# Norm sums added tile by tile under the projection slabs, in a two-layer hybrid block and a third block on one core

## The reference

```
def hybrid_layer(x, ...):
    z = rms_norm(x, norm_g) @ w_in
    y_conv = conv_module(...) @ w_conv_out          # 31 taps over time, LayerNorm, silu
    y_ret  = retention_branch(...) @ w_ret_out      # 4 heads, 256 x 512 each
    y_attn = window_attention_branch(...) @ w_attn_out
    merged = g[:, :, 0] * y_conv + g[:, :, 1] * y_ret + g[:, :, 2] * y_attn
    return x + merged @ w_out

def second_block(x, ...):
    h = _layer_norm(x, ln0_g, ln0_b)
    u_r, v_r, q_r, f_r, i_r, g_r, ga_r, gb_r = split(h @ w_in + b_in)
    y_a = _gmlp_spatial_gate(gelu(u_r), gelu(v_r), ...)   # LayerNorm over gelu(v_r)
    y_b = _hgrn2(q_r, f_r, i_r, g_r, ...)                 # 8 heads
    merged = sigmoid(ga_r) * (y_a @ w_a) + sigmoid(gb_r) * (y_b @ w_b)
    h1 = _layer_norm(ALPHA * h + merged @ w_o, ln1_g, ln1_b)
    ffn = (silu(h1 @ w_ffn_gate) * (h1 @ w_ffn_up)) @ w_ffn_down
    ple = sigmoid(h1 @ w_ple_gate + b_ple_gate) * (p @ w_ple)
    return _layer_norm(ALPHA * h1 + ffn + ple, ln2_g, ln2_b)
```

## Time and profile before

| what | us |
|---|---|
| median of 3 runs (3377.92 to 3380.22) | 3378.5 |
| the profiled execution | 3380.46 |
| its span | 3378.7 |
| TensorE busy in it | 3233.1 (96%) |
| VectorE, ScalarE, GpSimd busy | 1661.4, 1130.7, 1320.7 |
| mean granted TensorE clock | 0.98 of full |

### The profile page before, as it was taken

One profiled execution on the slowest core, in us unless ns is written; L12 is line 12 of the kernel. 1 busy time (PEld: TensorE's weight loads), 2 busy tenths in 40 slices (PEclk: granted clock), 3 DMA queues, 4 the chain that ended last, 5 costly groups with the idle time before them and its releaser, 6 DMA issues.

```text
span 3378.7 us, 42669 instructions
## 1 busy us (share of the span) xinstructions
PE 3233.1 (96%) x14040; PEld 2523.7 (75%) x14040; DVE 1661.4 (49%) x2500; ACT 1130.7 (33%) x1623; POOL 1320.7 (39%) x966
## 2 busy tenths in 40 slices
PE   7999999999999899999999999998999999999998
PEld 5866776767888686776776788876878787688885
DVE  5964565465344397575556544146562152331213
ACT  3232333355332222332235634224454232232222
POOL 3433433411555253433342145442334344254542
PEclk9999999999999999999999999998999999999999
DMA  4212222200322222221221032231112222132221
GB/s 150 97 63 68 87 66 71 71 29 29 122 100 93 96 102 67 88 69 67 75 75 44 26 106 94 99 118 49 63 68 75 87 88 93 62 100 98 94 98 70
DMA packets 73172, 272.07 MB, mean 81 GB/s; under 512 B 8128, under 2 KB 9152, under 8 KB 72384
## 3 DMA queue, kind: packets, MB, share of 16 engines
q1 hardware_dynamic: 69984, 252.74, 22.3%
q10 hardware_dynamic: 3072, 17.82, 1.5%
HBM read 264.24 MB, written 8.39 MB: 81 GB/s over the span
## 4 chain that ended last, share of the span: by engine, by line
PE 90%; DVE 5%; ACT 2%; DVEq 2%; issue 1%; DMA 0%; ACTq 0%; POOL 0%; SPq 0%; POOLq 0%
PE gem L296 22%; PE gem L298 22%; PE gem L297 22%; PE xp L382 4%; PE xp L541 2%; PE xp L372 2%; PE gem L504 2%; PE gem L638 1%; PE gem L639 1%; PE gem L640 1%; PE xp L511 1%; PE gem L484 1%; PE xp L647 1%; PE xp L615 1%; DVE U L1625 1%
## 5 line engine op out<-in xcount | busy, mean ns | idle before, releaser
L266 POOL TENSOR_TENSOR wlo<-raw,whi 128x512 fp32r<-128x512 f32 x956 | 1319.9, 1402 | 2013.9 <-ACT whi L779 2013.3
L296 PE MATMUL gem<-hhi,whi 128*128 128x512 f32 x2320 | 935.1, 403 | 4.5 <-POOL wlo L266 3.7
L298 PE MATMUL gem<-hhi,wlo 128*128 128x512 f32 x2320 | 905.0, 390 | 0.0
L297 PE MATMUL gem<-hlo,whi 128*128 128x512 f32 x2320 | 903.9, 390 | 0.0
L779 ACT ACTIVATE whi<-raw 128x1024 fp32r<-128x1024 f32 x478 | 504.3, 1055 | 663.6 <-PE gem L298 567.5
L296 PEld LDWEIGHTS gem<-hhi,whi 128*128 128x128 f32 x2320 | 436.4, 188 | 109.5 <-issue 17.4
L297 PEld LDWEIGHTS gem<-hlo,whi 128*128 128x128 f32 x2320 | 436.5, 188 | 104.5 <-issue 16.3
L298 PEld LDWEIGHTS gem<-hhi,wlo 128*128 128x128 f32 x2320 | 436.1, 188 | 91.8
L296 PE MATMUL gem<-zhi,whi 128*128 128x512 f32 x1008 | 396.8, 394 | 16.1 <-DVE zlo L1338 9.4
L297 PE MATMUL gem<-zlo,whi 128*128 128x512 f32 x1008 | 395.2, 392 | 0.0
L298 PE MATMUL gem<-zhi,wlo 128*128 128x512 f32 x1008 | 394.7, 392 | 0.0
(11 more groups left out here) (231 smaller groups left out, 3474.0 us busy)
## 6 DMA issues: line engine op xcount, KB each, us to landing
raw<-in_slabs SPq DMA_DIRECT2D x478, 512.0 KB, 3.4
U<-xsave ACTq DMA_DIRECT2D x2, 2048.0 KB, 8.1
xsave<-U ACTq DMA_DIRECT2D x2, 2048.0 KB, 7.5
U<-in_x ACTq DMA_DIRECT2D x1, 2048.0 KB, 9.5
out_y<-yr SPq DMA_DIRECT2D x8, 256.0 KB, 2.0
tab<-in_tab_ret ACTq DMA_DIRECT2D x2, 512.0 KB, 7.8
tab<-in_tab_att ACTq DMA_DIRECT2D x2, 512.0 KB, 3.6
tab<-in_tab_hg ACTq DMA_DIRECT2D x1, 512.0 KB, 8.0
```

The lines of the kernel that those rows point to most:

```text
L266: part = pool.tensor_tensor(wlo[:, k % 4, c], raw[:, k % 2, c], whi[:, k % 4, c].bitcast(f32), O.subtract)
L296: pe.matmul(o, wh, hi, start=(n == 0), stop=False)
L297: pe.matmul(o, wh, lo, start=False, stop=False)
L298: mm = pe.matmul(o, wl, hi, start=False, stop=(n == len(terms) - 1))
```

## The change

- x is loaded by SyncE in four pieces between the first two slabs, and ScalarE squares its tiles between its first copies. The copy of x to `xsave[0]` goes; layer 0 reloads x from its input. Vectors and tables are loaded further ahead.
- Every RMS norm: squares are added up by VectorE (`add_square`, tiles 0 to 6 into TT[2]), and TensorE does two all-ones matmuls (`square_sum`) in place of eight. In layer 0 the squares and additions of the next norm stand among the eight `w_out` slabs.
- LayerNorms 0, 2 and 3 (`ln_tiles`, `ln_shifted`): after four tiles their mean is taken (`mean_sum`, after slab 4), and all tiles are centred on it. Squares and the sum of the last four centred tiles are taken as the slabs come. What is left of the mean is subtracted afterwards (`shift`), and its square (DSQ) from the variance (VAR). Scale and shift move to ScalarE (`affine`). LayerNorm 1 keeps its exact mean, with one and two matmuls.
- LayerNorm 2's last sums stand between PLE slab 0 and 1; the read of PLE 1 stands between the affines.
- LayerNorm 0 has the copy of the block's slab 3 between its affines.
- In `gates`, `o_read` 0 and 1 stand before the tick of slab 3.
- The loop over the two layers and the last loops of the slabs before the norms are written out.

```diff
@@ gates @@
                     for k in range(4):
+                        if k == 3:
+                            o_read(hd, 0)
+                            o_read(hd, 1)
                         tick(G, k)
                         act.wait_ge(z_ready, L * 40 + hd * 4 + PRIMED)
                         read(k, SG[:, k, :], A.Silu)
-                        if k == 3:
-                            log_exp()
-                            o_read(hd, 0)
-                            o_read(hd, 1)
+                    log_exp()
@@ sync @@
-            for s in range(2):
-                sp.dma_start(raw[:, s, :], W[s]).then_inc(raw_in[s], 16)
+            sp.dma_start(raw[:, 0, :], W[0]).then_inc(raw_in[0], 16)
+            for i in range(4):
+                sp.dma_start(XN[:, 2 * i:2 * i + 2, :], ins["x"][:, 2 * i:2 * i + 2, :]).then_inc(x_first[i], 16)
+            sp.dma_start(raw[:, 1, :], W[1]).then_inc(raw_in[1], 16)
@@ tensor @@
+            def square_sum(n, bank):
+                pe.wait_ge(sq_sum, n + 1)
+                pe.matmul(xp[:, bank, :], ones[:, :], TT[:, 2, :], start=True, stop=False)
+                pe.wait_ge(sq_ready, 8 * n + 8)
+                pe.matmul(xp[:, bank, :], ones[:, :], TT[:, 1, :], start=False, stop=True).then_inc(ssq, 1)
+            def mean_sum(n):
+                pe.wait_ge(ln_part, n + 1)
+                pe.matmul(xp[:, 0, :], ones[:, :], TT[:, 3, :], start=True, stop=True).then_inc(ln_mean, 1)
+            def shifted_sums(n, last):
+                pe.wait_ge(ln_rest, (0, None, 1, 2)[n] + 1)
+                pe.matmul(xp[:, 1, :], ones[:, :], TT[:, 3, :], start=True, stop=False)
+                pe.wait_ge(ln_cent, 8 * n + 8)
+                pe.matmul(xp[:, 1, :], ones[:, :], last, start=False, stop=True).then_inc(ln_off, 1)
+                square_sum(DEPTH + n, 2)
@@ scalar @@
+            LN_TURNS = ((), (), (), (), (), (0, 1, 2, 3), (4,), (5, 6, 7))
+            def shifted_root(n):
+                act.wait_ge(ln_off, (0, None, 1, 2)[n] + 1)
+                act.activation(DSQ, xp[:, 1, :], A.Square, scale=1.0 / D).then_inc(ln_dsq, 1)
+                act.wait_ge(ln_var, (0, None, 1, 2)[n] + 1)
+                inv_sqrt(RS, VAR, 1.0, EPS5, rstd)
...
+            log_exp()
+            high(0, 0, False)
+            for i in range(NT):
+                if i % 2 == 0:
+                    act.wait_ge(x_first[i // 2], 16)
+                square(0, i, XN[:, i, :])
+                if i == 3:
+                    high(0, 1, False)
+            high(0, 2, False)
...
+            tick(Gp, 0)
+            for j in range(4):
+                read(j, PL[:, j, :], A.Copy)
+            shifted_root(2)
+            for i in range(NT):
+                if i == 2:
+                    tick(Gp, 1)
+                    for j in (2, 3, 0, 1):
+                        read(j, PL[:, 4 + j, :], A.Copy)
+                affine(2, i, XC[:, i, :], B_LN1)
@@ vector, ln_tiles (the last tiles) @@
+                for i in range(5):
+                    center(i)
+                for i in (1, 2, 3):
+                    add_square(DEPTH + n, i)
+                make(5)
...
+                make(7)
+                dve.drain()
+                center(7)
@@ vector, ln_shifted @@
+                stt(VAR, xp[:, 2, :], 1.0 / D, DSQ, O.mult, O.subtract).then_inc(ln_var, 1)
+                shift(0)
...
+                shift(3)
+                dve.drain()
+                dve.wait_ge(rstd, DEPTH + n + 1)
+                for i in range(NT + 1):
+                    if i < NT:
+                        tt(src(i), src(i), RS, O.mult).then_inc(ln_mul, 1)
+                    if i < 4:
+                        shift(4 + i)
+                    if each and i:
+                        dve.wait_ge(ln_out, (0, None, 8)[n] + i)
+                        each(i - 1)
```

## The result

The changed kernel takes 3275.5 us (median of 4 runs, 3272.1 to 3277.6), the kernel before 3378.2 beside it: ratio 0.969, interval 0.968 to 0.971. The forecast was 3275. The profiled execution took 3273.6, its span 3271.8, so 106.9 less than the span of before. The mean granted clock rose from 0.980 to 0.984 of full. That is some 135 us at half clock before and 105 after, so at most some 15 us of the gain are clock.

What follows compares the result with a forecast made beforehand. TensorE was taken as the bound, so only less TensorE work, standstill or half clock could help. Seven terms sum to 103.7 us; off the median that gives 3274.8, predicted 3275, range 3258 to 3303.

Steps and rivals of the forecast that it cites:

- value products: Heads of both layers: copies sooner remove eight 2.6 us waits (20.8) and 8 us of low clock; together 29 us less.
- norm of the gated values: Block's norm of gated values: one and two all-ones matmuls are left of 16; 13.3 us less, bounds 10 and 14.
- start: Program start to first matmul: x in pieces, squares following them, two all-ones matmuls; 7 us less, bounds 4 and 10.
- layer boundary: Last product of layer 0 to next gemm: squares and additions run under slabs, 7.1 us remain; 15.5 us less.
- first LayerNorm of block two: Last product to first gemm read: 30.4 us instead of 41.9, 1.9 of it GpSimd's interference; 11.5 us less.
- second LayerNorm: Product to first gate slab's read: 37.3 us instead of 52.2, three slabs starting at 19; 15 us less.
- end: Last product to end of span, through the final norm: 18.6 us against 30.9; 12.4 us less, bounds 11 and 13.
- The sign that I had named for it: At the start: the step is wrong if squares 4 to 7 end well after 18 us; forecast near 17.2.
- nothing waits for it: Norm of the gated values: claimed that nothing waits for this norm, only its all-ones sums counting, 13.3 us less.
- The thin reserve: Norm of the gated values: weight copy behind the eight squares has wlo done at 2645, needed at 2647.7; reserve 2.7 us.
- The clock as the larger part (2): Whole kernel: with less standing still TensorE stays at 2.4 GHz, time 3260 us or below; chance 10%.
- the 9 us of the forecast's rule: Three norms: VectorE with two SBUF inputs and GpSimd lock one another out; would lose 9 us, time 3284; 1.9 taken instead.

Runs made afterwards that it cites:

- the three runs: Changed kernel with o_read 0 and 1 late again: 3303.0 us; kernel before with only them early: 3348.8; kernel before with unused matmuls in those waits: 3370.4.

## Why the prediction was right, and where it wasn't

The total was right to a microsecond, the terms less so; errors of both signs cancelled, and that is luck. Two of the seven terms lie outside their own bounds, the value products and the norm of the gated values, both above. In the two attention parts the clock gave 3.6 and took 4.6, by the chance of these two executions.

| term | forecast | by the table of leads |
|---|---|---|
| start | 7 (4 to 10) | 4.2 |
| value products | 29 (19 to 31) | 17.8 + 14.8 = 32.6 |
| layer boundary | 15.5 (13 to 16.5) | 15.4 |
| first LayerNorm of block two | 11.5 (8 to 13.5) | 12.9 |
| norm of gated values | 13.3 (10 to 14) | 15.9 |
| second LayerNorm | 15 (11 to 17) | 15.3 |
| end | 12.4 (11 to 13) | 11.8 |
| attention of the two layers (not in the sum) | 0 | 3.6 and -4.6 |
| other slabs (not in the sum) | 0 | about -0.4 |

**Start.** The failed step is "squares follow the pieces ... VectorE's last addition near 17.5". The sign that I had named for it came: the last square ends at 20.70, not near 17. I counted the bytes on the queues, and slab 1 did land where they say (14.09 where nothing else holds its copy up). I did not count that VectorE's first addition stands behind its wait for the six constants (1.3 us, by the sums' start at 19.64 and not 20.96 without it), nor that ScalarE's squares need VectorE to free their buffer, so that squares and additions take turns, two of these additions stretched by GpSimd from 0.69 to 1.35 and 1.58 (1.6 us together). Going through the new order engine by engine and asking what each first instruction waits for would have brought it up. The sums, the root and the first tile (20.96 to 28.47, 7.5 us) were as forecast (7.3).

**Value products.** The mechanism was right in both halves, as the three runs show. Mis-sized were the clock, 8 for 9.7, and the wait: counted from the modelled end of a matmul it is 2.60, but from start to start it is 205.85 - 202.87 = 2.98, where 0.23 is usual, so 2.75, or 22.0 for eight. 22.0 + 9.7 = 31.7 of the 32.6. The row of before on which that rests:

```profile
202.87 0.39 PE L298 MATMUL gem<-hhi,wlo 128*128 128x512 f32 x1
```

**Boundary and ends of norms.** 7.27 against 7.1, 11.7 against 11.6 to the block's first matmul, 19.6 against 19 and 37.1 against 37.3 in the second LayerNorm, 7.64 against 7.65 to the last norm's first multiply: adding the rows of a chain up, engine by engine, works to 0.6 us. The end came 0.6 later. Half of it is VectorE's four rounds, 1.37 each for 1.3; the rest is ScalarE, whose scaling with scale and shift of its own for each partition took 0.81 and not the 0.67 of my row (0.73 each in the last four, behind multiplies of 0.61).

**First LayerNorm of block two.** The number was near (29.6 for 30.4), the reason wrong: tiles stretched by GpSimd were to set it, and the low clock does (at full clock the tiles come next, and 0.5 us is all that is won). And 4.7 us of the gain are handed back at once: the lead reaches 70.6 in the slab after it and is 65.9 behind it, as TensorE now waits 9.3 where it waited 4.6 (L665 in the waits above), for VectorE's work for the first head, which doesn't come sooner by as much. My term ended at the read of slab 0 and didn't ask who is late next.

**Norm of the gated values.** The failed step is "nothing waits for it". In the kernel before TensorE stood still for 2.00 us ahead of the sums of squares, until ScalarE's first square:

```profile
2661.10 7.30 PE L615 MATMUL xp<-U,ones 128*128 128x512 f32 x12 [2.00 <-ACT U L1031]
```

From start to start (2658.71 to 2661.10) that is 2.2 more than usual, and 13.3 + 2.2 is 15.5 of the 15.9. The thin reserve held: in the changed kernel the last square ends at 2574.6 and TensorE doesn't wait for the copy behind it.

**Rivals.** The clock as the larger part (2) was given 10%. It is out: of the 106.9 us at most some 15 are clock, half of the time at half clock that is gone (135 before, 105 after). That 18.7 us more come when pauses are filled shows how much is left in it: the changed kernel still has its pauses. GpSimd did stretch splits and additions on VectorE, but in the norms behind slabs the additions lie under slabs, where nobody waits for them, and after the last product GpSimd is idle until the next copy: the 9 us of the forecast's rule did not come. Only at the start, where no slab covers them, did additions pay, the 1.6 us above. That rule of the Trainium skill (SBUF — State Buffer, "SBUF: two separate sides") agrees with the rows (1.61 for 0.69); its price was small here.

## What to carry to other kernels

Add up a norm's chain between two gemms row by row, from the last product to the first matmul, and ask at each removed wait what is next and at each new first instruction which older waits stand ahead of it. A pause of TensorE can cost twice, once itself and once in the clock behind it (in five of eight heads here); where nothing can be moved into the pause, matmuls nobody needs can keep the clock up, and here they paid where TensorE was the bound behind the pause. With effects of some microseconds compare the starts of the same instructions around the edit: the same code elsewhere differed by up to 5 us between executions.

## What the runs showed of the hardware

- Matmuls of 128 columns by all ones in the pauses held the granted clock at 1.00 in nine of ten stretches of 12 to 18 us where it had been 0.68 to 0.86, and raised its mean from 0.984 to 0.996; ten of them in each pause of 2.6 us were worth 9.7 us in eight heads.
- Pauses at the same instruction were followed by half-clock stretches of other lengths in other executions of one kernel (clock 0.74 and 0.87 in one stretch, 0.70 and 0.80 in another), and in one place by none in one execution and 6.8 us in the other (1.00 and 0.79).
- A matmul of 128 columns took 0.23 us in a row of 30 at full clock (6.86 us for 30), and 0.28 in a row of 30 that began 1.00 us into the program (8.49 for 30).
- A VectorE copy (one input) was stretched beside GpSimd as well, 0.75 and 1.35 for 0.43; additions with two inputs took 1.35 and 1.58 for 0.69.
